# The residual behind w_o turned without its norm, and the norm factor multiplied in later

## The chip, the core and the metric

The kernel runs on one core of a Trainium2 chip. The metric is the device time of one execution in microseconds (us), taken as the median of several executions. All arithmetic is fp32; matrix products are made from split operands, described below.

## What is computed

Two transformer blocks run on 256 tokens of width 2048. The change lies at the end of the second block:

```python
x = x + mixed @ w_o[l]
x = x + peer(rmsnorm(x, norm_ffn_g[l]), peer_wq[l], peer_keys1[l], peer_keys2[l], peer_u[l], peer_v[l])

def rmsnorm(x, g):
    y = x * rsqrt(mean(x * x, axis=-1) + EPS)      # one factor per token
    return y * g                                   # one gain per column

def peer(x, wq, keys1, keys2, u, v):               # per token, 8 heads
    q = x @ wq;  s1 = q[first half] @ keys1;  s2 = q[second half] @ keys2
    # top 16 of s1 and of s2, their 256 sums, top 16 of these: expert numbers and scores
    gate = softmax(top scores)
    act = gelu(x @ u[expert]) * gate
    return act @ v[expert]
```

The kernel does not gather the rows of `u` and `v`. It multiplies all 16,384 experts, as 128 blocks of 128, and puts the gates into a table of tokens and experts that is zero elsewhere. The norm factor of a token (`rstd` below) is one number by which a whole row of x is multiplied, so it can also be multiplied into the scores and into `x @ u` afterwards.

## The kernel before, in words

**Products.** TensorE (PE) multiplies with operands in fp32r, each split in a high and a low part. A stream of 902 units of weights (128x1024) is loaded by the SP queue into four slots. ScalarE (ACT) copies a unit into `w_hi` (`split_hi`, L488), VectorE (DVE) subtracts into `w_lo` (`split_lo`, L497), and PE takes both. Two units are a pair. `ahead` (L507) makes the splits two pairs before PE needs them, and a slot can be split again only when PE has finished the pair that used it. `tokens_out` (L585) makes a 512-column block of a product with tokens on the partitions; `halves_out` (L552) makes a 128-column block with columns on the partitions, first `w_hi` against both activation parts (L561), then `w_lo` against the high part (L568). The stages follow the stream: ..., `heads`, `w_o`, `wqu` (router: per head two pairs of queries and two pairs of expert blocks), `u_decode`, `u_gates`, `u_late`, `v`.

**w_o.** PE makes four column blocks of x (`mix_block`, L2549) in banks 0 to 3. DVE adds each to the residual X (`add_blocks`, L1651), and ACT sums the squares of a block while PE makes the next. In the last block, one token half is finished first, so that its sum, root and reciprocal (`add_last`, `mean_last`, `root_last`, L1931 to L1949) run beside the other half.

**The norm, before.** When w_o has ended, `norm_last` (DVE, L1951) and `norm_second` (ACT, L1113) multiply X by `rstd` into XN, PE turns XN (32 transposes of 128x128, `turn_ffn`, L2588), and ACT and DVE multiply by the gain and split into `act_hi` and `act_lo` (`keep_ffn_hi` L1117, `keep_ffn_lo` L1955). The first query product waits for them tile by tile (`paced` in `halves_out`). The same turning is done earlier in the kernel without the norm, block by block between products, by `turn_block` (L2249), `keep_hi_tiles` (L784) and `keep_lo_tiles` (L1358): the stages w_out and gate use it, and there the norm factor goes into a later step.

**Router.** Per head, ACT copies the queries from their bank and GpSimd (POOL) adds their two halves (`add_copied`, L727, L729); PE multiplies with the keys (`query_scores`, L2615), ACT copies the scores (L1160), and DVE takes the top 16 of each (`top16`, L1983). The two expert blocks of the turn are added on POOL too, and ACT applies Gelu and stores them (`save_early`, L1144).

**u_decode.** 16 expert blocks, numbered 0 to 15 here. Meanwhile DVE turns the picked numbers into expert numbers (L2032 to L2087), with the work of the blocks put between these steps (`more`, L2025): a unit's `split_lo`, and after every second one `add_halves` (L576, L579), which adds the two halves of a block. For a block, ACT waits for this sum, applies Gelu and starts a store (`save_decoded`, L1193), and only then copies the next block's low half (`low_half`, L572) and splits the second unit that DVE wants next. PE starts block n when the sum of block n-2 is made (L2640).

**Scatter.** When the picks are ready, POOL writes the gates of the second 128 tokens into the table in HBM with 128 indirect DMAs (L742). SP waits for all of them before it loads on at the beginning of `u_late` (L642), since it loads the table there.

```python
for n in range(2):                                   # u_decode on ACT, L1182 to L1191
    ahead(split_hi, act, "u_decode", i, 2, n, units=(0,))
    save_decoded(i, n - 1)                           # waits for the sum, Gelu, store
    ...
    low_half(act, GZ[:, n, :], banks[2 + n])
    ahead(split_hi, act, "u_decode", i, 2, n, units=(1,))
```

Of the kernel before, what the change touches and what calls it, by code (L numbers as in the profile page):

```python
# [139 lines left out]
def build(nc, stream, x, p_t, rows, consts, params, rg_w, ukv, keys_t, out):  # L140
    ctx = ExitStack()
    with ctx:
# [108 lines left out]
        RSTD_ROW = at(32512, S)  # L251
        IWORK = at(6200, TT * S).rearrange("p (t n) -> p t n", t=TT)
# [111 lines left out]
        normed_s = sem("normed_s")  # L364
# [169 lines left out]

        def ffn_chunk(k):
            return banks[(4, 5, 6, 7, 2, 3, 1, 4)[k // 2]][:, k % 2 * S:k % 2 * S + S]
# [134 lines left out]
        def _(pool):  # L671
# [58 lines left out]

            with pool.Fori(0, PH) as h:
                for a in range(2):
                    pool.wait_ge(ps_made[a], h + 1)
                    add_copied(PQS[:, a, :], QUERY_HALVES[:, a, :], h * 4 + a)
                for n in range(2):
                    add_copied(Z_HALVES[:, n, 0:S], Z_HALVES[:, n, :], h * 4 + (2 + n))
# [16 lines left out]
        def _(act):  # L753
# [154 lines left out]
            def split_and_square(part, base, i):  # L908

                for k in range(15 if part == "w_o" else 16):  # L910
                    ahead(split_hi, act, part, 0, 8, k)
                    if part == "w_out" and k == 6:

                        act.wait_ge(softplus_ready, 1)
                        act.activation(sp_b, sp_a, ACT.Exp, scale=-1.0).then_inc(softplus_ready, 1)
                    if k >= 4 and k % 4 == 1:
                        if part == "w_out":
                            keep_hi_tiles(1, pa("gate_gain"), gate_in_hi, k // 4 - 1)
                        block_squares(added, base, k // 4 - 1)
# [184 lines left out]
            for t in range(TT):  # L1104
                act.wait_ge(added[1], 8 + t)
                act.activation(XN[:, t, 1536:2048], X[:, t, 1536:2048], ACT.Square,
                               accum_out=ss4[:, 4 * t + 3:4 * t + 4]).then_inc(squares, 1)
                act.wait_ge(mean_ready, 5 + t)
                act.activation(std[:, t:t + 1], ss[:, t:t + 1], ACT.Sqrt).then_inc(std_ready, 1)
                if not t:  # L1110
                    ahead(split_hi, act, "w_o", 0, 8, 15, units=(0,))

            def norm_second(cc):  # L1113
                cols = slice(cc * 512, (cc + 1) * 512)
                act.activation(XN[:, 1, cols], X[:, 1, cols], ACT.Copy, scale=rstd[:, 1:2]).then_inc(normed_s, 1)

            def keep_ffn_hi(chunks):  # L1117
                gain = pa("ffn_gain")
                for k in chunks:
                    act.wait_ge(turned, 3 * KT + k // 2 * 2 + 2)  # L1120
                    act.activation(act_hi[:, k, :], ffn_chunk(k), ACT.Copy, scale=gain[:, k:k + 1])\
                       .then_inc(act_hi_ready, 1)
# [30 lines left out]
            def router_turn(h, first=False):  # L1153
                def keep_query(a):
                    copy_halves(QUERY_HALVES[:, a, :], banks[a], pair_of("wqu", h, 4, a), h * 4 + a, 4)

                def keep_scores(a):
                    act.wait_ge(ps_made[a], h + 2)
                    act.wait_ge(ps_used[a], h + 1)
                    act.activation(PS[:, a, :, :].rearrange("p t n -> p (t n)"), banks[4 + a][:, 0:S],  # L1160
                                   ACT.Copy).then_inc(ps_kept[a], 1)

                ahead(split_hi, act, "wqu", h, 4, 0)
                keep_query(0)
# [3 lines left out]
                keep_query(1)  # L1168
                keep_scores(0)
# [23 lines left out]
            def save_decoded(i, n):  # L1193
                wait_summed(act, block_of("u_decode", i, 2, n))
# [21 lines left out]
            def save_gelu(i, n):  # L1216
                wait_summed(act, block_of("u_gates", i, 2, n))
# [27 lines left out]
            def late_turn(i, first=False):  # L1245
                for n in range(2):
# [9 lines left out]
                    wait_summed(act, block_of("u_late", i, 2, n))  # L1256
# [80 lines left out]
        def _(dve):  # L1337
# [313 lines left out]
            def add_blocks(part, first_banks=(0, 2)):  # L1651

                for b in range(4):
                    n = b % 2
                    for k in range(3):
                        ahead(split_lo, dve, part, 0, 8, 4 * b + k)
                        if part == "w_out" and b and k == 1:
                            keep_lo_tiles(2, pa("gate_gain"), gate_in_hi, gate_in_lo, b - 1)
                        if part == "w_out" and (b, k) == (1, 2):
                            softplus()  # L1660
# [290 lines left out]
            def norm_last(t, cc):  # L1951
                cols = slice(cc * 512, (cc + 1) * 512)
                dve.tensor_scalar(XN[:, t, cols], X[:, t, cols], rstd[:, t:t + 1], None, ALU.mult).then_inc(normed, 1)

            def keep_ffn_lo(chunks):  # L1955
                gain = pa("ffn_gain")
                for k in chunks:
                    dve.wait_ge(act_hi_ready, 4 * KT + k // 2 * 2 + 2)
                    dve.scalar_tensor_tensor(out=act_lo[:, k, :], in0=ffn_chunk(k), scalar=gain[:, k:k + 1],
                                             in1=act_hi[:, k, :].bitcast(F32), op0=ALU.mult, op1=ALU.subtract)\  # L1960
                       .then_inc(act_lo_ready, 1)

# [4 lines left out]
            dve.wait_ge(added[1], 8)  # L1967
            norm_last(0, 0)
            add_last(1)
            for cc in range(1, 4):  # L1970
                norm_last(0, cc)
            mean_last(1)
            root_last(1)
            dve.wait_ge(added[1], 9)
            norm_last(1, 0)
            norm_last(1, 1)
            keep_ffn_lo(range(8))
            ahead(split_lo, dve, "w_o", 0, 8, 15, units=(0,))
            keep_ffn_lo(range(8, 16))
# [132 lines left out]

            def gates_turn(i, last=False):
                for n in range(2):
# [5 lines left out]
                    add_gates(i, n)  # L2120

# [5 lines left out]
            with dve.Fori(GATED, EARLY // 2 - 2 * PH) as i:  # L2127
                for n in range(2):
                    ahead(split_lo, dve, "u_gates", i, 2, n)
                    add_halves(dve, GZ[:, n, :], banks[2 + n], block_of("u_gates", i, 2, n))  # L2130
            for n in range(2):
# [3 lines left out]
            def late_turn(i):  # L2135
                for n in range(2):
                    ahead(split_lo, dve, "u_late", i, 2, n)
                    add_halves(dve, GZ[:, n, :], banks[2 + n], block_of("u_late", i, 2, n))
                    dve.wait_ge(gelu_ready[n], i + (EARLY // 2 + 1) + 1)
# [95 lines left out]
        def _(pe):  # L2235
# [13 lines left out]
            def turn_block(turn, b, taken):  # L2249
                pe.wait_ge(taken[b % 2], b // 2 * 2 + 3)  # L2250
# [313 lines left out]
            mix_block(0, 1)  # L2564
            pe.wait_ge(added[0], 7)
            mix_block(1, 0)
            pe.wait_ge(added[1], 7)
            mix_block(1, 1, range(6))
# [19 lines left out]
            def turn_ffn(t, chunks):  # L2588
                for k in chunks:
                    ins = pe.transpose(ffn_chunk(k)[:, t * P:(t + 1) * P], XN[:, t, k * P:(k + 1) * P], ident)  # L2590
                    if t:
                        ins.then_inc(turned, 1)

            pe.wait_ge(added[0], 9)
            for cc in range(4):
                pe.wait_ge(normed, 4 + cc + 1)
                if cc == 3:
                    pe.wait_ge(added[1], 9)
                turn_ffn(0, range(4 * cc, min(4 * cc + 4, 14)))
            for cc in range(2):  # L2600
                pe.wait_ge(normed, 8 + cc + 1)
                turn_ffn(1, range(4 * cc, 4 * cc + 4))
            pe.wait_ge(normed_s, 1)
            turn_ffn(1, range(8, 12))
            pe.wait_ge(normed_s, 2)
            turn_ffn(1, range(12, 14))
            pe.wait_ge(act_lo_ready, 4 * KT + 2)
            turn_ffn(0, range(14, 16))
            turn_ffn(1, range(14, 16))

            def queries_out(h, a, paced=False):
                pe.wait_ge(copied, h * 4 + (a + 1))
                halves_out(pe, pair_of("wqu", h, 4, a), odd_of("wqu", a), banks[a], paced=4 * KT if paced else None)
# [12 lines left out]
            queries_out(0, 0, paced=True)  # L2626
            queries_out(0, 1)
            pe.wait_ge(table_ready, 32)
# [215 lines left out]
```

## Time and profile before

| | us |
|---|---|
| three runs of the kernel | 2696.3, 2696.33, 2696.57 (median 2696.33) |
| the profiled execution | 2696.89 |
| its span, first to last instruction | 2695.2 |
| PE busy in the span | 2669.4 (99%) |
| DVE busy | 1835.3 (68%) |
| ACT busy | 1369.4 (51%) |
| POOL busy | 371.4 (14%) |

The times below are in us from the start of the span of the profiled execution. A line of the timeline gives a start, a length, the engine, the line of the kernel, what is written from what, how many instructions are merged, and in brackets how long the engine stood idle before and who ended that. Lengths of PE overlap, since matmuls are pipelined; what a matmul costs is read from one start to the next. The span is 1.7 below the execution's own time.

### The profile page before, as it was taken

The numbers are of one execution on the slowest core, as the hardware profiler recorded it, in microseconds if no ns is written. First come the engines' busy times: TensorE is split into PE (matmuls) and PEld (weight loads), VectorE is DVE, ScalarE is ACT, GpSimd is POOL, SyncE is SP. The second block draws the span as 40 slices with busy tenths as digits, with TensorE's granted clock in tenths as the row PEclk, the third lists the DMA queues.
The fourth block names the chain that finished last, engine by engine and source line by source line (L and its number), as shares of the span: only waits on it lengthen the run. The fifth ranks groups of instructions, "written<-read, shape, count | busy, mean of one in ns | idle before, by whom it ended". The sixth has DMA issues, their size and how long they took to land.

```text
span 2695.2 us, 47112 instructions
## 1 busy us (share of the span) xinstructions
PE 2669.4 (99%) x14299; PEld 2298.4 (85%) x14299; DVE 1835.3 (68%) x2985; ACT 1369.4 (51%) x2066; POOL 371.4 (14%) x296
## 2 busy tenths in 40 slices
PE   8999999999999999999999999999999999999998
PEld 6888888898888998888888888888888888888887
DVE  6666665668987677489996777775565555555555
ACT  6454445555665444455455555554444444444444
POOL 0010000001011211011105555551000000000000
PEclk9999999999999999999999999999999999999999
DMA  7566555564554554655567777777976666666564
GB/s 257 189 216 213 181 199 177 177 219 159 172 176 156 167 168 157 195 201 186 195 201 212 202 202 203 201 204 218 305 240 217 217 217 219 212 220 216 200 241 156
DMA packets 204475, 543.26 MB, mean 202 GB/s; under 512 B 37504, under 2 KB 82816, under 8 KB 203392
## 3 DMA queue, kind: packets, MB, share of 16 engines
q1 hardware_dynamic: 148112, 486.74, 54.9%
q10 hardware_dynamic: 35568, 47.33, 5.0%
q0 software_dynamic: 20736, 8.46, 2.7%
q8 instruction: 30, 0.49, 0.1%
q14 instruction: 29, 0.24, 0.0%
HBM read 515.12 MB, written 27.33 MB: 201 GB/s over the span
## 4 chain that ended last, share of the span: by engine, by line
PE 94%; DVE 3%; ACT 1%; issue 1%; DMA 0%; SPq 0%; DVEq 0%; POOL 0%; ACTq 0%; POOLq 0%
PE bank L561 32%; PE bank L568 16%; PE bank L2693 8%; PE bank L2694 8%; PE bank L2695 8%; PE bank L601 4%; PE bank L603 4%; PE bank L602 4%; PE bank L2488 1%; DVE w_lo L504 1%; PE bank L527 1%; PE bank L528 1%; PE bank L529 1%; PE bank L2658 1%; PE bank L2465 0%
## 5 line engine op out<-in xcount | busy, mean ns | idle before, releaser
L504 DVE TENSOR_TENSOR w_lo<-raw,w_hi 128x1024 fp32r<-128x1024 f32 x902 | 1097.9, 1226 | 725.9 <-ACT w_hi L495 719.4
L495 ACT ACTIVATE w_hi<-raw 128x1024 fp32r<-128x1024 f32 x902 | 950.8, 1059 | 946.5 <-PE bank L568 363.1
L561 PE MATMUL bank<-act,w_hi 128*128 128x512 f32 x3840 | 975.2, 396 | 2.6 <-DVE cst L579 1.0
L561 PEld LDWEIGHTS bank<-act,w_hi 128*128 128x128 f32 x3840 | 692.0, 189 | 133.8 <-issue 6.4
L568 PEld LDWEIGHTS bank<-act,w_lo 128*128 128x128 f32 x3840 | 519.7, 190 | 33.1
L568 PE MATMUL bank<-act,w_lo 128*128 128x256 f32 x3840 | 535.6, 282 | 0.0
L2693 PE MATMUL bank<-w_hi,expert_act 128*128 128x512 f32 x1008 | 392.3, 389 | 0.1
L2694 PE MATMUL bank<-w_lo,expert_act 128*128 128x512 f32 x1008 | 392.2, 389 | 0.0
L2695 PE MATMUL bank<-w_hi,expert_act 128*128 128x512 f32 x1008 | 392.1, 389 | 0.0
L742 POOL DMA_INDIRECT g_kept<-slot_t x128 | 239.7, 1872 | 253.8 <-issue 170.4
L2693 PEld LDWEIGHTS bank<-w_hi,expert_act 128*128 128x128 f32 x1008 | 189.3, 188 | 39.6 <-DVE cst L579 0.5
L2695 PEld LDWEIGHTS bank<-w_hi,expert_act 128*128 128x128 f32 x1008 | 189.3, 188 | 39.3
L2694 PEld LDWEIGHTS bank<-w_lo,expert_act 128*128 128x128 f32 x1008 | 189.3, 188 | 39.1
L601 PE MATMUL bank<-w_hi,act 128*128 128x512 f32 x320 | 125.8, 393 | 2.0 <-DVE act L1401 1.1
L603 PE MATMUL bank<-w_hi,act 128*128 128x512 f32 x320 | 124.7, 390 | 0.0
L602 PE MATMUL bank<-w_lo,act 128*128 128x512 f32 x320 | 124.6, 389 | 0.0
L748 POOL TENSOR_TENSOR big<-big 128x1024 f32<-128x1024 f32 x2 | 5.8, 2878 | 839.4 <-DVE big L2196 839.4
L601 PEld LDWEIGHTS bank<-w_hi,act 128*128 128x128 f32 x320 | 60.1, 188 | 16.2 <-DVE w_lo L504 1.3
L603 PEld LDWEIGHTS bank<-w_hi,act 128*128 128x128 f32 x320 | 60.1, 188 | 12.6
L602 PEld LDWEIGHTS bank<-w_lo,act 128*128 128x128 f32 x320 | 60.1, 188 | 12.1
L729 POOL TENSOR_TENSOR big<-big 128x256 f32<-128x256 f32 x32 | 33.1, 1034 | 248.3 <-ACT big L1138 248.3
L2107 DVE SCALAR_TENSOR_TENSOR weighted<-cst,slot_t 128x256 fp32r<-128x256 f32 x128 | 61.3, 479 | 0.0
(344 smaller groups left out, 2498.4 us busy)
## 6 DMA issues: line engine op xcount, KB each, us to landing
raw<-in_stream SPq DMA_DIRECT2D x902, 512.0 KB
z_kept<-cst ACTq DMA_DIRECT2D x112, 128.0 KB, 2.4
cst<-z_kept ACTq DMA_DIRECT2D x112, 128.0 KB, 3.9
g_kept<-zeros POOLq DMA_DIRECT2D x16, 512.0 KB
big<-in_ukv ACTq DMA_DIRECT2D x16, 512.0 KB, 4.6
big<-g_kept SPq DMA_DIRECT2D x16, 512.0 KB, 5.6
big<-in_rows ACTq DMA_DIRECT2D x3, 1024.0 KB, 5.8
big<-in_x SPq DMA_DIRECT2D x2, 1024.0 KB, 10.2
```

Source lines behind the costliest of these rows:

```text
L495: act.activation(w_hi[:, s, :], raw[:, s, :], ACT.Copy).then_inc(hi_ready, 1)
L504: dve.tensor_tensor(w_lo[:, s, :], raw[:, s, :], w_hi[:, s, :].bitcast(F32), ALU.subtract).then_inc(lo_ready, 1)
L561: pe.matmul(bank[:, :], w_hi[:, s, kk * P:(kk + 1) * P], act2[:, k, :, :].rearrange("p a n -> p (a n)"), start=(k == 0), stop=False)
L568: mm = pe.matmul(bank[:, 0:S], w_lo[:, s, kk * P:(kk + 1) * P], act_hi[:, k, :], start=False, stop=(k == KT - 1))
L601: pe.matmul(outs[t], a_hi, hi, start=(k == 0), stop=False)
L602: pe.matmul(outs[t], a_hi, lo, start=False, stop=False)
L603: mm = pe.matmul(outs[t], a_lo, hi, start=False, stop=(k == KT - 1))
L742: pool.indirect_dma_start(g_kept, bass.IndirectOffsetOnAxis(ap=SLOT_INDEX[:, i:i + 1], axis=0), SLOT_GATE[:, i:i + 1], None, compute_op=AL ...
L2107: dve.scalar_tensor_tensor(out=weighted[:, tile, :, :], in0=iota.unsqueeze(1).broadcast_to([P, 2, P]), scalar=first_index[:, bass.ds(tok, 1)],
L2693: pe.matmul(o, a_hi, hi, start=first, stop=False, skip_group_check=True)
L2694: pe.matmul(o, a_hi, lo, start=False, stop=False, skip_group_check=True)
L2695: mm = pe.matmul(o, a_lo, hi, start=False, stop=False, skip_group_check=True)
```

## The change

- `norm_last`, `norm_second`, `turn_ffn`, `keep_ffn_hi` and `keep_ffn_lo` go. X itself is turned by `turn_block`: blocks 0, 1 and 2 in the middle of w_o's next block, block 3 between the two units of the first query pair (`first_queries`). ACT and DVE keep its tiles with `keep_hi_tiles` and `keep_lo_tiles`, blocks 0 to 2 during w_o, block 3 behind it. On ACT and DVE the first unit of the pair after the first query pair is now split before block 3's tiles.
- DVE makes two diagonals of `rstd`; PE multiplies them with ones, which gives a row of `rstd` on every partition (two matmuls between the second query pair and the first scores), and ACT keeps it as `FFN_ROW`.
- Scores are multiplied by `rstd` while ACT copies them, in two instructions per copy instead of one.
- Expert blocks are multiplied by `FFN_ROW` (128x256) before Gelu: on POOL in the router and in `u_decode`, on DVE in `u_gates` and `u_late`. ACT waits for the multiplied block. POOL's loop over `u_decode` stands ahead of the scatter.

```diff
+            def early_block(n, block):
+                z = Z_HALVES[:, n, 0:S]
+                pool.wait_ge(copied, block + 5)
+                step(pool.tensor_tensor(z, z, Z_HALVES[:, n, S:2 * S], ALU.add))
+                pool.wait_ge(row_kept, 2)
+                step.wait()
+                pool.tensor_tensor(z, z, FFN_ROW, ALU.mult).then_inc(pool_summed, 1)
...
+            with pool.Fori(0, PH) as i:
                 for n in range(2):
-                    add_copied(Z_HALVES[:, n, 0:S], Z_HALVES[:, n, :], h * 4 + (2 + n))
+                    wait_summed(pool, block_of("u_decode", i, 2, n))
+                    pool.tensor_tensor(GZ[:, n, :], GZ[:, n, :], FFN_ROW, ALU.mult).then_inc(z_scaled, 1)
             pool.wait_ge(picks_ready, 5)
...
-            act.wait_ge(rstd_ready, 7)
-            norm_second(2)
-            keep_ffn_hi(range(4))
-            norm_second(3)
-            keep_ffn_hi(range(4, 8))
+            ahead(split_hi, act, "w_o", 0, 8, 15, units=(0,))
+            keep_hi_tiles(3, pa("ffn_gain"), act_hi, 3)
             ahead(split_hi, act, "w_o", 0, 8, 15, units=(1,))
-            keep_ffn_hi(range(8, 16))
...
-                    act.activation(PS[:, a, :, :].rearrange("p t n -> p (t n)"), banks[4 + a][:, 0:S],
-                                   ACT.Copy).then_inc(ps_kept[a], 1)
+                    for t in range(TT):
+                        kept = act.activation(PS[:, a, t, :], banks[4 + a][:, t * P:(t + 1) * P], ACT.Copy,
+                                              scale=rstd[:, t:t + 1])
+                    kept.then_inc(ps_kept[a], 1)
...
             def save_decoded(i, n):
-                wait_summed(act, block_of("u_decode", i, 2, n))
+                act.wait_ge(z_scaled, i * 2 + (n + 1))
...
             ahead(split_lo, dve, "w_o", 0, 8, 15, units=(0,))
-            keep_ffn_lo(range(8, 16))
+            keep_lo_tiles(4, pa("ffn_gain"), act_hi, act_lo, 3)
+            step(dve.memset(ONES, 1.0))
+            for t in range(TT):
+                step(dve.tensor_scalar(RSTD_DIAG[:, t, :], ident, rstd[:, t:t + 1], None, ALU.mult))
+            step.wait()
+            dve.sem_inc(rstd_ready, 1)
             ahead(split_lo, dve, "w_o", 0, 8, 15, units=(1,))
...
+            def scale_rows(n, block):
+                wait_summed(dve, block)
+                dve.tensor_tensor(GZ[:, n, :], GZ[:, n, :], FFN_ROW, ALU.mult).then_inc(z_scaled, 1)
...
-            mix_block(0, 1)
+            mix_block(0, 1, range(4))
+            turn_block(2, 0, added, 4)
+            mix_block(0, 1, range(4, 8))
...
+            def first_queries():
+                pe.wait_ge(copied, 1)
+                pe.wait_ge(added[1], 8)
+                pe.wait_ge(act_lo_ready, 4 * KT + 12)
+                halves_out(pe, pair_of("wqu", 0, 4, 0), odd_of("wqu", 0), banks[0], units=(0,))
+                turn_block(2, 3, added, 4)
+                halves_out(pe, pair_of("wqu", 0, 4, 0), odd_of("wqu", 0), banks[0], units=(1,), paced=4 * KT)
...
+            pe.wait_ge(rstd_ready, 8)
+            for t in range(TT):
+                ins = pe.matmul(banks[6][:, t * P:(t + 1) * P], ONES, RSTD_DIAG[:, t, :], start=True, stop=True)
+            ins.then_inc(row_made, 1)
```

## Rows read from the trace of the kernel before

**Rows 1.** Stretches: length, then busy time of PE, PEld, DVE, ACT, POOL (instructions), clock, DMA.

```profile
1152.30:1166.20 13.90, 11.28 (x65) 8.38 (x65) 12.15 (x29) 10.49 (x24) 0.00 (x0) 1.00 0.45 164
1166.20:1346.60 180.40, 180.40 (x1058) 159.46 (x1057) 160.10 (x445) 91.55 (x124) 32.33 (x31) 1.00 0.59 196
1346.60:1438.75 92.15, 91.06 (x518) 79.34 (x516) 79.77 (x105) 55.20 (x77) 12.91 (x8) 1.00 0.68 205
1438.75:1625.00 186.25, 186.25 (x1088) 164.57 (x1087) 138.22 (x257) 99.32 (x160) 102.11 (x56) 1.00 0.74 203
1900.50:1990.50 90.00, 90.00 (x520) 79.28 (x519) 56.90 (x81) 45.49 (x66) 0.00 (x0) 1.00 0.90 289
```

**Rows 2.** Timeline of PE from w_o's last product to the second query pair.

```profile
1151.92 0.39 PE L2582 MATMUL bank<-w_hi,mix_lo 128*128 128x512 f32 x1
...
1158.86 2.28 PE L561 MATMUL bank<-act,w_hi 128*128 128x512 f32 x8
...
1166.20 2.00 PE L561 MATMUL bank<-act,w_hi 128*128 128x512 f32 x8
```

**Rows 3.** Timeline of PE in w_out: a block of eight transposes between products.

```profile
400.90 0.40 PE L603 MATMUL bank<-w_hi,act 128*128 128x512 f32 x1
401.14 1.04 PE L2256 MATMUL bank<-cst,big 128*128 128x128 f32 x8
401.93 0.47 PE L601 MATMUL bank<-w_hi,act 128*128 128x512 f32 x1
```

**Rows 4.** Timeline of ACT and DVE behind w_o: the last root, and four tiles on each.

```profile
1154.54 0.20 ACT L1109 ACTIVATE stat<-stat 128x1 f32<-128x1 f32 x1 [0.72 <-DVE stat L1943]
1155.99 1.57 ACT L1121 ACTIVATE act<-bank,par 128x256 fp32r<-128x256 f32 x4 [0.30 <-PE bank L2590]
1156.87 1.66 DVE L1959 SCALAR_TENSOR_TENSOR act<-bank,par,act 128x256 fp32r<-128x256 f32 x4 [1.01 <-ACT act L1121]
```

**Rows 5.** Timeline of PE: the first scores and the product behind them.

```profile
1171.79 0.61 PE L2620 MATMUL bank<-big 128*128 128x128 f32 x4
1172.15 2.09 PE L561 MATMUL bank<-act,w_hi 128*128 128x512 f32 x8
```

**Rows 6.** Waits of DVE in the router, 1166 to 1346: total, times, longest.

```profile
DVE w_lo L504 <- ACT w_hi L495: 13.3, 24, 1.6
```

**Rows 7.** Timeline of DVE and PE in u_decode.

```profile
1357.70 0.42 DVE L579 TENSOR_TENSOR cst<-cst,bank 128x256 f32<-128x256 f32 x1
1361.89 2.28 DVE L2053 TENSOR_TENSOR big<-big,cst 128x2048 f32<-128x2048 f32 x1
1409.83 0.41 DVE L579 TENSOR_TENSOR cst<-cst,bank 128x256 f32<-128x256 f32 x1
1410.38 2.10 PE L561 MATMUL bank<-act,w_hi 128*128 128x512 f32 x8 [0.15 <-DVE cst L579]
```

**Rows 8.** Timeline of ACT in u_decode: Gelu of a block, then the next split.

```profile
1380.03 0.42 ACT L1195 ACTIVATE cst<-cst 128x256 f32<-128x256 f32 x1 [0.85 <-DVE cst L579]
...
1381.41 1.06 ACT L495 ACTIVATE w_hi<-raw 128x1024 fp32r<-128x1024 f32 x1
```

**Rows 9.** Timeline of POOL and DVE where both are busy, in the rnn stage.

```profile
621.83 2.39 POOL L701 TENSOR_TENSOR ckvt_lo<-big,ckvt_hi 128x1024 fp32r<-128x1024 f32 x1 [320.72 <-DVE big L1772]
622.25 3.05 DVE L504 TENSOR_TENSOR w_lo<-raw,w_hi 128x1024 fp32r<-128x1024 f32 x1
...
624.18 1.62 POOL L706 TENSOR_TENSOR big<-big 128x256 f32<-128x256 f32 x1
```

**Rows 10.** Lines L719 and L742 on POOL and L504 on DVE: length min/median/max in ns, first and last start.

```profile
L719 POOL TENSOR_TENSOR big<-big x32: 734/738/742, 818.5 to 1068.2; 128x256 f32<-128x256 f32 x32
L504 DVE TENSOR_TENSOR w_lo<-raw,w_hi x902: 1203/1225/3053, 5.9 to 2678.0; 128x1024 fp32r<-128x1024 f32 x181
L742 POOL DMA_INDIRECT g_kept<-slot_t x128: 1552/1576/2657, 1416.6 to 1841.3; - x128
```

**Rows 11.** Timeline of SP: the first load behind its wait for the scatter.

```profile
1878.76 0.34 SPq L619 DMA_DIRECT2D raw<-in_stream  x1
```

More of the change, by code:

```diff
@@ L729, in add_copied @@
                 pool.tensor_tensor(dest, halves[:, 0:S], halves[:, S:2 * S], ALU.add).then_inc(pool_summed, 1)
-            with pool.Fori(0, PH) as h:
-                for a in range(2):
-                    pool.wait_ge(ps_made[a], h + 1)
-                    add_copied(PQS[:, a, :], QUERY_HALVES[:, a, :], h * 4 + a)
+            def early_block(n, block):
[5 more added lines that the diff above has]
+                pool.tensor_tensor(z, z, FFN_ROW, ALU.mult).then_inc(pool_summed, 1)
+            with pool.Fori(0, PH) as h:
+                with step.turns(h, 2, PH):
+                    for a in range(2):
+                        pool.wait_ge(ps_made[a], h + 1)
+                        add_copied(PQS[:, a, :], QUERY_HALVES[:, a, :], h * 4 + a)
+                    for n in range(2):
+                        early_block(n, h * 4 + (2 + n))
+            with pool.Fori(0, PH) as i:
                 for n in range(2):
-                    add_copied(Z_HALVES[:, n, 0:S], Z_HALVES[:, n, :], h * 4 + (2 + n))
+                    wait_summed(pool, block_of("u_decode", i, 2, n))
+                    pool.tensor_tensor(GZ[:, n, :], GZ[:, n, :], FFN_ROW, ALU.mult).then_inc(z_scaled, 1)
             pool.wait_ge(picks_ready, 5)
@@ L1168, in router_turn @@
                 keep_query(1)
+                if first:
+                    act.wait_ge(row_made, 2)
+                    act.activation(FFN_ROW, banks[6][:, 0:S], ACT.Copy).then_inc(row_kept, 1)
+                    act.wait_ge(rstd_ready, 7)
                 keep_scores(0)
@@ L1658, in add_blocks @@
                             keep_lo_tiles(2, pa("gate_gain"), gate_in_hi, gate_in_lo, b - 1)
+                        if part == "w_o" and b and k == 1:
+                            keep_lo_tiles(4, pa("ffn_gain"), act_hi, act_lo, b - 1)
                         if part == "w_out" and (b, k) == (1, 2):
@@ L1949, in root_last @@
                 dve.wait_ge(rstd_ready, 6 + t)
[L1951 to L1961, printed above, removed]
             dve.wait_ge(added[0], 9)
@@ L2120, in gates_turn @@
                     add_gates(i, n)
+                    scale_rows(n, block_of("u_gates", i, 2, n))
             dve.wait_ge(scattered, 16 * ZERO_DMAS)
@@ L2130, in _ @@
                     add_halves(dve, GZ[:, n, :], banks[2 + n], block_of("u_gates", i, 2, n))
+                    scale_rows(n, block_of("u_gates", i, 2, n))
             for n in range(2):
@@ L2138, in late_turn @@
                     add_halves(dve, GZ[:, n, :], banks[2 + n], block_of("u_late", i, 2, n))
+                    scale_rows(n, block_of("u_late", i, 2, n))
                     dve.wait_ge(gelu_ready[n], i + (EARLY // 2 + 1) + 1)
@@ L2563, in _ @@
             pe.wait_ge(added[1], 5)
-            mix_block(0, 1)
+            mix_block(0, 1, range(4))
+            turn_block(2, 0, added, 4)
+            mix_block(0, 1, range(4, 8))
             pe.wait_ge(added[0], 7)
-            mix_block(1, 0)
+            mix_block(1, 0, range(4))
+            turn_block(2, 1, added, 4)
+            mix_block(1, 0, range(4, 8))
             pe.wait_ge(added[1], 7)
-            mix_block(1, 1, range(6))
+            mix_block(1, 1, range(4))
+            turn_block(2, 2, added, 4)
+            mix_block(1, 1, range(4, 6))
             pair = pair_of("w_o", 0, 8, 15)
@@ L2586, in _, with queries_out @@
                     mm.then_inc(bank_done, 1)
[L2588 to L2611, printed above, removed]
-                pe.wait_ge(copied, h * 4 + (a + 1))
-                halves_out(pe, pair_of("wqu", h, 4, a), odd_of("wqu", a), banks[a], paced=4 * KT if paced else None)
+            def queries_out(h, a):
+                pe.wait_ge(copied, h * 4 + (a + 1))
+                halves_out(pe, pair_of("wqu", h, 4, a), odd_of("wqu", a), banks[a])
+            def first_queries():
[5 more added lines that the diff above has]
+                halves_out(pe, pair_of("wqu", 0, 4, 0), odd_of("wqu", 0), banks[0], units=(1,), paced=4 * KT)
             def query_scores(h):
```

36 lines of the change are left out of this document (9 added, 27 removed).

## The prediction, made before the changed kernel was run

> **What bounds the kernel now.** The page comes first: PE is busy in nearly the whole span, so a change is worth what it takes from, or adds to, PE's path. The table of stretches says where that isn't so. PE has no idle time in the router, in u_gates and in u_late; between w_o and the router it is idle for 2.6 of 13.9 us, and in u_decode for 1.1 of 92.15 us [rows 1]. The change touches exactly these two places: it shortens the first and puts a step into the second. The timeline of the first shows w_o's last product at 1151.92 and the second query pair at 1166.20 [rows 2]. The timeline of the second shows DVE without a pause, and a PE that waits 0.15 us for a block's sum by DVE [rows 7]: there DVE sets the pace, not PE.
>
> Terms are differences within the profiled execution (2696.89 us, 0.56 above the median of the runs); I add them to the median, 2696.33. A measurement of this kernel can tell some 0.2%, 5.4 us, from no change.
>
> **1. What goes behind w_o.** Products start 0.24 apart [rows 3], so w_o leaves PE at 1152.16; up to 1166.20 are 14.04 us. The first query pair in it needs what the second takes, 1166.20 to 1171.79, 5.59 us [rows 2, 5]. Saved: 8.45 us, the 32 transposes, the waits for the norm and the paced tiles together.
>
> **2. What comes in its place.** A block of eight transposes between products costs 0.79 from its start to the next product's, which is 0.07 longer than usual [rows 3]: 0.86. Three blocks in w_o: 2.6. They wait for nothing: a block of X is summed half a w_o block earlier, and w_out does the same now. ACT's and DVE's twelve tiles there take 0.39 and 0.42 each [rows 4], beside PE. The fourth block costs 0.86 and holds up the second half of the query pair: root at 1154.54, then ACT's split of 1.06 [rows 4, 8], which now stands before the tiles, then DVE's of 1.23 [rows 10], then four tiles of 0.42. That puts the last tile at 1158.3 (DVE's norm steps ahead of the root are gone) to 1158.7, and the pair's end some 1.3 later (its last product and its low half, an estimate), at 1159.6 to 1160.0, against 1152.16 + 5.59 + 0.86 = 1158.6 without a wait. I take 1.1, bounds 0 (the engines get there first) and 2.5 (both chains one after the other). The two matmuls for the row of factors cost what two such matmuls of the scores do, 0.36 plus 0.09 of the next product [rows 5]: 0.45. Sum: 8.45 - 2.6 - 0.86 - 1.1 - 0.45 = **3.4 saved**, between 2.0 and 4.5.
>
> **3. Edits costed at nothing.** Scores in two ACT instructions, and the router's second POOL step per block: ACT is busy for half of the router, and DVE still waits 13.3 us for ACT's splits there [rows 1, 6], 1.7 per head; POOL's step may take some 1 us of that from DVE. Were that cover gone, it would be up to 8 us. DVE's 0.42 per block in u_gates and u_late: DVE is busy for 138.2 of 186.25 and 56.9 of 90 us [rows 1], and what waits for the scaled block, Gelu, is wanted only a pair later. SP's queue is not moved.
>
> **4. What the change adds in u_decode.** ACT's Gelu now waits for DVE's sum and then POOL's multiplication. The shape on POOL takes 0.74 [rows 10]. This is short, but it does not run beside DVE. In the rnn stage POOL subtracts for 2.39 us; DVE's split, begun meanwhile, takes 3.05 instead of 1.23, and POOL's next step, behind that split, takes 1.62 [rows 9, 10] for a shape that elsewhere takes 0.74. Each waits until the other has finished, and the one that waits goes first. The Trainium skill says the same on its page "SBUF — State Buffer", section "Who interferes with whom": a VectorE instruction with two SBUF inputs and a GpSimd instruction that reads SBUF exclude each other, and the second to issue is blocked until the first has finished. By that rule each multiplication costs DVE most of its own length, and the sum is the one below; without it, it is the first rival's. The 3.05 and the 1.62 agree with it.
>
> DVE's work here is such instructions, one behind another: splits, the comparison of 2.28 (L2053), products. From the sum of block 0 to that of block 9, 1357.70 to 1409.83, it does not rest [rows 7]. After each of the nine sums before the last, POOL stands behind DVE's next instruction, then holds the one after it. I take 0.6 for each (0.74 less the overlap that instructions have): 5.4. After block 0, DVE's split waits for ACT's, which waits for Gelu: 0.2 more than the hold; and after the four L2053 POOL starts 2.2 late, Gelu with it, and ACT's split is done 2.44 after Gelu's start [rows 8], just when DVE wants it: 0.4 in all. DVE's chain comes **6.0** later to block 9's sum, and PE, which waits for that sum today [rows 7], too. From block 10 on the picks are nearly done and DVE has pauses again. Bounds: 0.8 (no collision, only the step's length, once) and 7.5 (nine full 0.74 and more of ACT's lateness).
>
> **Sum:** 6.0 - 3.4 = +2.6. Forecast **2698.9 us**; by the bounds of both terms, 2696.3 to 2701.8. This is no change that can be measured, made of two that could nearly be.
>
> **Rivals.** *No collision.* POOL's reads don't hold DVE's products (only splits are seen to be held [rows 9]), or DVE's chain has more air than it seems. Then u_decode costs 0.8 to 1.5 and the time is 2693.8 (2692 to 2695.5). For it: sums of blocks on POOL in the router leave no mark on PE. Against: rows 9.
>
> *DVE keeps the port: slower.* If POOL gets in only when DVE stops, then after L2053 nothing but two-input instructions follows until DVE waits for the split that hangs on POOL. Place: blocks 1, 3, 5, 7. Price: 0.74 + 2.44 of rest each, 12.7, and some 3.3 for the others: 16 in place of 6, so 2709. It decides if POOL is passed over once per block. Against: in rows 9 the engine that waited was served first, though there it was DVE.
>
> *The scatter comes too late: slower.* POOL's loop over u_decode now stands before it. It began at 1416.6; it can begin when block 15 is multiplied, some 4 us behind the end of u_decode at 1438.75 [rows 1], so 26 later. It ended its last start at 1841.3 [rows 10], some 5 us before it had landed (estimate); with 26 more, 1872. SP's load behind the wait goes out at 1878.76 [rows 11]: 6 us of room, and about 6 more until PE misses the unit. It decides if the scatter's 425 us become 3% longer; at 5%, 9 us: 2708.
>
> *The fourth block costs as much as the norm did.* Then the first term is 0 to 1 and the time 2702.
>
> **How the numbers follow.** Forecast 0.50, no collision 0.26, DVE keeps the port 0.11, late scatter 0.04, fourth block 0.04, 0.05 for a gain I don't see. The range of 2692 to 2703 leaves out the third, the fourth and the last, 0.20; the forecast's own is 2696.3 to 2701.8. Faster than 2690.9 needs more than the whole bound of the first term: 0.06. Slower than 2701.7: the three slow rivals and the edge of the forecast, 0.20. Within: 0.74.
>
> **What would show it.** Right: the second query pair begins some 7.8 us behind the start of w_o's last product (0.24 + 5.59 + 0.86 + 1.1), where it was 14.3; w_o is 2.6 longer; in u_decode DVE instructions with two SBUF inputs are 0.6 longer behind each sum, POOL's multiplication takes 0.7 to 3 us, and block 0 to block 9 takes 58 us instead of 52.1; PE waits for L579 more than now. Wrong: L2053, L2062 and L504 keep their lengths in u_decode (no collision); DVE idle for 3 us before L504 at every second block (port kept); SP waiting for the scatter near 1879; or PE idle behind w_o for more than 2.5 us.

## The result, and the profile of the changed kernel

The changed kernel takes 2700.15 us (median of 19 runs, the shortest 2699.07), the one before 2696.42: a ratio of 1.0019, 95% interval 1.0013 to 1.0025. This is 3.7 us, where 2.6 were forecast, and less than the 5.4 us by which "no change" was bounded. It is the case that the prediction called likeliest: a gain behind w_o and a larger loss in u_decode. The profiled execution took 2699.15 us (span 2697.5). Four of the 19 runs, called long below, took 2706.22 to 2711.17 us, and one of the kernel before 4458.5, so medians are compared.

First the table of stretches, cut at the same places of the work as [rows 1] (behind w_o up to the second query pair, router, u_decode, u_gates; columns as there):

```profile
1153.85:1161.36 7.51, 7.19 (x41) 5.69 (x40) 5.08 (x13) 5.34 (x10) 0.00 (x0) 1.00 0.39 156
1161.36:1342.25 180.89, 180.89 (x1062) 159.94 (x1061) 160.89 (x446) 95.76 (x141) 43.97 (x46) 1.00 0.60 202
1342.25:1440.64 98.39, 92.05 (x518) 79.50 (x517) 86.11 (x105) 54.98 (x77) 22.91 (x17) 1.00 0.58 191
1440.64:1627.26 186.62, 186.35 (x1088) 164.56 (x1087) 148.68 (x288) 99.35 (x160) 102.66 (x56) 1.00 0.74 203
```

Behind w_o 7.51 us stand where 13.90 stood, and PE is idle for 0.32 of them, not for 2.6. u_decode takes 98.39 instead of 92.15, and PE, which was idle for 1.1 us of it, now is for 6.3.

The timeline of PE behind w_o, which answers to [rows 2] and [rows 5]:

```profile
1153.62 0.39 PE L2583 MATMUL bank<-w_hi,mix_lo 128*128 128x512 f32 x1
1153.85 1.98 PE L559 MATMUL bank<-act,w_hi 128*128 128x512 f32 x8
...
1156.62 1.04 PE L2251 MATMUL bank<-cst,big 128*128 128x128 f32 x8
1157.41 1.17 PE L559 MATMUL bank<-act,w_hi 128*128 128x512 f32 x4
1158.89 1.68 PE L559 MATMUL bank<-act,w_hi 128*128 128x512 f32 x4 [0.32 <-DVE act L1365]
...
1161.36 2.00 PE L559 MATMUL bank<-act,w_hi 128*128 128x512 f32 x8
...
1166.95 0.61 PE L2616 MATMUL bank<-big 128*128 128x128 f32 x4
1167.40 0.61 PE L2606 MATMUL bank<-big 128*128 128x128 f32 x4
```

The last product of w_o begins at 1153.62, the second query pair at 1161.36: 7.74 us, where the prediction said 7.8 and the kernel before took 14.3. The fourth block's transposes stand at 1156.62 and the one wait for its tiles at 1158.89. The two matmuls for the row of factors take 0.45, from 1166.95 to the first scores.

Then u_decode. DVE's timeline, from the sum of block 0 to that of block 9 (L577 is the sum, L505 the split, L2041 and L2050 the comparison and the products), which answers to [rows 7]; POOL's own; and the split and the products of the kernel before:

```profile
1353.31 0.41 DVE L577 TENSOR_TENSOR cst<-cst,bank 128x256 f32<-128x256 f32 x1
...
1371.77 2.28 DVE L2041 TENSOR_TENSOR big<-big,cst 128x2048 f32<-128x2048 f32 x1
1373.97 1.76 DVE L505 TENSOR_TENSOR w_lo<-raw,w_hi 128x1024 fp32r<-128x1024 f32 x1
1375.65 1.28 DVE L2050 TENSOR_TENSOR big<-big 128x512 f32<-128x512 f32 x2
1377.18 1.22 DVE L505 TENSOR_TENSOR w_lo<-raw,w_hi 128x1024 fp32r<-128x1024 f32 x1 [0.25 <-ACT w_hi L496]
1378.32 0.41 DVE L577 TENSOR_TENSOR cst<-cst,bank 128x256 f32<-128x256 f32 x1
1378.65 1.83 DVE L2050 TENSOR_TENSOR big<-big 128x512 f32<-128x512 f32 x2
...
1411.72 0.41 DVE L577 TENSOR_TENSOR cst<-cst,bank 128x256 f32<-128x256 f32 x1
```

```profile
1371.93 2.72 POOL L747 TENSOR_TENSOR cst<-cst,par 128x256 f32<-128x256 f32 x1 [5.43 <-DVE cst L577]
1378.81 1.12 POOL L747 TENSOR_TENSOR cst<-cst,par 128x256 f32<-128x256 f32 x1 [4.17 <-DVE cst L577]
```

```profile
1376.10 1.22 DVE L504 TENSOR_TENSOR w_lo<-raw,w_hi 128x1024 fp32r<-128x1024 f32 x1
...
1379.91 1.29 DVE L2062 TENSOR_TENSOR big<-big 128x512 f32<-128x512 f32 x2
```

Block 0 to block 9 takes 58.41 us; it was 52.13. Read the first two fences together. POOL is released by the sum and issues at 1371.93, 0.16 behind the start of L2041; it ends only at 1374.65, for it stands still until L2041 is done. Now the split of 1373.97 stands still for POOL: 1.76 in place of 1.22. In the next block POOL meets a product, whose pair takes 1.83 in place of 1.28. Each of the first nine multiplications holds DVE for some 0.55 us; this is called a hold below. Five times DVE also waits for ACT's split, as at 1377.18, because Gelu came late: 0.22, 0.27, 0.25, 0.25 and 0.24. The Gelu ahead of that split was released by POOL:

```profile
1374.68 0.42 ACT L1196 ACTIVATE cst<-cst 128x256 f32<-128x256 f32 x1 [4.75 <-POOL cst L747]
```

The waits of 1340 to 1460 (total, times, longest) say the same from the other side; behind them, PE's in the same stretch of the kernel before:

```profile
ACT cst L1196 <- POOL cst L747: 30.1, 14, 4.8
...
PE bank L559 <- DVE cst L577: 6.2, 8, 1.0
```

```profile
PE bank L561 <- DVE cst L579: 1.0, 4, 0.4
```

Last, the scatter on POOL, its first and its last start, and SP's first load behind the wait for it, which answer to [rows 10] and [rows 11]; and the one wait of ACT for that load:

```profile
1444.79 1.80 POOL L753 DMA_INDIRECT g_kept<-slot_t  x1 [0.22 <-issue]
...
1882.66 2.50 POOL L753 DMA_INDIRECT g_kept<-slot_t  x1 [0.30 <-issue]
```

```profile
1886.74 0.81 SPq L617 DMA_DIRECT2D raw<-in_stream  x2
```

```profile
ACT w_hi L496 <- DMA raw<-in_stream: 1.9, 1, 1.9
```

The scatter starts 28.2 us later and its last DMA 41.4 later, for it also takes 437.9 us from first to last start where it took 424.7. SP's load was due at 1881.0 (1878.76, and 2.26 for the later place of the whole kernel) and goes out at 1886.74. ACT waits 1.9 us for what it brings; PE has no wait there yet.

### The profile page after: what moved, and what is told of

Its sections match the earlier page's. It is cut to its first block, busy times and chain, and to the rows that moved or that the text cites. A ratio compares the mean times of both kernels' runs of the same rounds, so it can differ in the third digit from the quotient of the medians.

```text
span 2697.5 us, 47398 instructions
## 1 busy us (share of the span) xinstructions
PE 2669.1 (99%) x14303; PEld 2299.3 (85%) x14303; DVE 1874.8 (70%) x3078; ACT 1372.0 (51%) x2081; POOL 407.3 (15%) x328
## 4 chain that ended last, share of the span: by engine, by line
PE 83%; issue 12%; POOL 2%; DVE 1%; ACT 1%; DMA 0%; POOLq 0%; SPq 0%; DVEq 0%; ACTq 0%
PE bank L559 26%; PE bank L566 14%; PE bank L2683 8%; PE bank L2685 8%; PE bank L2684 8%; PE bank L599 4%; PE bank L601 3%; PE bank L600 3%; PE bank L2483 1%; PE bank L528 1%; PE bank L529 1%; PE bank L530 1%; POOL big L727 1%; POOL big L732 1%; PE bank L2648 1%
## 5 line engine op out<-in xcount | busy, mean ns | idle before, releaser
L505 DVE TENSOR_TENSOR w_lo<-raw,w_hi 128x1024 fp32r<-128x1024 f32 x902 | 1100.4, 1230 | 687.7 <-ACT w_hi L496 670.8
L2143 DVE TENSOR_TENSOR expert_act<-big,expert_act 128x256 fp32r<-128x256 f32 x128 | 53.6, 420 | 0.8 <-ACT expert_act L1263 0.8
```

The costliest lines, as they stand in the source:

```text
L505: dve.tensor_tensor(w_lo[:, s, :], raw[:, s, :], w_hi[:, s, :].bitcast(F32), ALU.subtract).then_inc(lo_ready, 1)
```

## Experiments

All are run beside the kernel before on the same chip; its median was 2696.4 to 2696.7 each time. The diffs show the lines that matter; `...` stands for lines left out, among them the counts of semaphores that follow from the edit. In experiments 1 to 4 and 7 the norm factor of u_decode's blocks is left out.

**1. Without the multiplication in u_decode.** POOL's loop is taken out, Gelu waits for the sum.

```diff
-    with pool.Fori(0, PH) as i:
-        for n in range(2):
-            wait_summed(pool, block_of("u_decode", i, 2, n))
-            pool.tensor_tensor(GZ[:, n, :], GZ[:, n, :], FFN_ROW, ALU.mult).then_inc(z_scaled, 1)
...
 def save_decoded(i, n):
-    act.wait_ge(z_scaled, i * 2 + (n + 1))
+    wait_summed(act, block_of("u_decode", i, 2, n))
...
```

> The changed kernel without the multiplication of u_decode's sixteen blocks by the row of factors; ACT's Gelu waits for DVE's sum again and POOL's scatter starts as soon as the picks are ready. It leaves out the norm factor of these blocks. My theory, that the part behind w_o gives 3.4 us and everything that is lost is lost in u_decode: block 0's sum to block 9's takes 52.1 us again instead of 58.4, the scatter starts some 4 us earlier than in the kernel before, and the time is 2693.0 (2692.0 to 2694.2), with no run some us above the others. Rival, that the late start is an accident of the profiled run and the part behind w_o gives nothing: 2696. Rival, that u_gates' and u_late's multiplications on DVE cost as well: 2694.5 or more.

Measured: 2693.16 us, ratio 0.9989 (0.9980 to 0.9998); block 0 to block 9 in 51.88 us. So the part behind w_o gives 3.3 us net in time (by the interval, 0.5 to 5.4), and the changed kernel loses through u_decode's multiplication. DVE's multiplications in u_gates and u_late show no cost.

**2. The same with the late scatter.** One wait more on POOL, for the sum of u_decode's last block.

> As the kernel without the multiplication in u_decode, but POOL waits for the sum of u_decode's last block before it scatters, as the changed kernel makes it. Norm factor of u_decode's blocks left out. If the late scatter is what made 4 of 19 runs of the changed kernel 6 to 11 us longer, then most runs stay within 1 us of the kernel without the multiplication (2693) and about one in five is 5 to 11 us above that; the scatter ends about 28 to 41 us later than with the early start. If those long runs have another cause (the multiplication itself, the first stages), no run here is more than 3 us above the median.

Measured: 2693.09 us, ratio 0.9987 (0.9978 to 0.9996), 11 runs from 2691.98 to 2693.87. The scatter began at 1437.85, 25 us later than in experiment 1, but its last start was at 1854.28, only 23 later, and SP's load was not held. No run is long, where the expectation had about one in five: by its own words this speaks for another cause of the long runs, though 11 runs are few.

**3. POOL beside DVE, nobody waiting.** On experiment 1, POOL multiplies the row of factors by itself into an unused tile after each of the first ten sums.

```diff
+    for k in range(10):
+        wait_summed(pool, block_of("u_decode", 0, 2, k))
+        pool.wait_ge(z_scaled, k)
+        pool.tensor_tensor(GB[:, k % 2, :], FFN_ROW, FFN_ROW, ALU.mult).then_inc(z_scaled, 1)
...
```

> As the kernel without the multiplication, but POOL multiplies two unrelated inputs of 128x256 into an unused tile after each of u_decode's first ten sums; nobody waits for it there. Norm factor of u_decode's blocks left out. My theory, that POOL and DVE hold each other: each of DVE's splits or products behind a sum is 0.55 longer, block 0's sum to block 9's takes 52.1 + 9 x 0.55 = 57.0 us, and the time is 2693.0 + 4.9 = 2697.9 (2696.5 to 2698.5). Rival, that what costs in u_decode is the longer chain from sum to Gelu and not the port: 52.1 to 52.7 us, DVE's instructions keep their lengths, 2693.0 to 2693.6.

Measured: 2697.33 us, ratio 1.0004 (0.9995 to 1.0013); block 0 to block 9 in 55.60. DVE's timeline and POOL's:

```profile
1371.51 2.28 DVE L2041 TENSOR_TENSOR big<-big,cst 128x2048 f32<-128x2048 f32 x1
1373.71 1.63 DVE L505 TENSOR_TENSOR w_lo<-raw,w_hi 128x1024 fp32r<-128x1024 f32 x1
1375.27 1.28 DVE L2050 TENSOR_TENSOR big<-big 128x512 f32<-128x512 f32 x2
...
1377.94 1.70 DVE L2050 TENSOR_TENSOR big<-big 128x512 f32<-128x512 f32 x2
```

```profile
1371.67 2.60 POOL L747 TENSOR_TENSOR cst<-par 128x256 f32<-128x256 f32 x1 [5.42 <-DVE cst L577]
1378.09 0.99 POOL L747 TENSOR_TENSOR cst<-par 128x256 f32<-128x256 f32 x1 [3.83 <-DVE cst L577]
```

The same two instructions are held, by 0.42 (1.63 and 1.70), with no wait for ACT anywhere between them: nine times 0.42 are 3.8 us, and the stretch grew by 3.7. My 4.9 was worked out with the 0.55 of the changed kernel. The rival, that only the longer chain costs, is out. That the hold is 0.42 and not 0.55 goes with POOL's own instruction, which takes 0.61 alone, not 0.74, when both inputs are the same tile. Nearly all that is left of the changed kernel's 6.28 is 9 x 0.13, or 1.2, and the 1.23 of waits for ACT.

**4. The same with one input.** As experiment 3, with a multiplication by a constant. This changes POOL's operation as well (TENSOR_SCALAR).

```diff
-        pool.tensor_tensor(GB[:, k % 2, :], FFN_ROW, FFN_ROW, ALU.mult).then_inc(z_scaled, 1)
+        pool.tensor_scalar(GB[:, k % 2, :], FFN_ROW, 2.0, None, ALU.mult).then_inc(z_scaled, 1)
```

> As the kernel with POOL's unrelated multiplication of two inputs, but POOL multiplies one input of 128x256 by a constant. Norm factor of u_decode's blocks left out. With two inputs DVE's next instruction was 0.42 longer, POOL's own 0.61 less some 0.19. If any read of SBUF by POOL holds DVE's two-input instructions: a hold of POOL's length less 0.19, block 0's sum to block 9's 51.9 + 9 times that, 2693.2 + the same less 0.7. If only POOL's two-input instructions hold: 51.9 us, DVE's lengths unchanged, 2693.2.

Measured: 2694.94 us, ratio 0.9994 (0.9985 to 1.0003); 53.71 us. Neither: DVE is held, but by 0.20 only, although POOL's instruction is the longest of the three (0.85 alone, and 1.23 behind a product). This run does not tell apart whether the number of inputs or the operation makes the hold short. The lines:

```profile
1373.63 1.42 DVE L505 TENSOR_TENSOR w_lo<-raw,w_hi 128x1024 fp32r<-128x1024 f32 x1
...
1377.64 1.48 DVE L2050 TENSOR_TENSOR big<-big 128x512 f32<-128x512 f32 x2
```

```profile
1377.80 1.23 POOL L747 TENSOR_SCALAR cst<-par 128x256 f32<-128x256 f32 x1 [3.38 <-DVE cst L577]
...
1408.82 0.85 POOL L747 TENSOR_SCALAR cst<-par 128x256 f32<-128x256 f32 x1 [4.97 <-DVE cst L577]
```

**5. The multiplication on DVE**, right behind each sum; the scatter starts early again. POOL's loop is taken out.

```diff
...
                     add_halves(dve, GZ[:, pair % 2, :], banks[2 + pair % 2], block_of("u_decode", 0, 2, pair))
+                    scale_rows(pair % 2, block_of("u_decode", 0, 2, pair))
...
```

> The changed kernel with u_decode's multiplication on DVE, right behind each sum, instead of on POOL; the scatter starts as soon as the picks are ready. My theory: DVE's chain gets 0.33 to 0.42 us for each of nine blocks and no holds; ACT's Gelu comes 0.4 later instead of 0.7 to 2.7, so little of the 0.25 waits stays: block 0's sum to block 9's takes 55.1 to 56.2 us instead of 58.4, the time is 2696.0 to 2697.3, and no run lies 5 us or more above the median if the late scatter made those. Rival, that the cost is the step itself wherever it runs: 58 us and 2699 to 2700.

Measured: 2698.44 us, ratio 1.0008 (0.9999 to 1.0017), 1.1 us above my range; block 0 to block 9 in 56.03, inside it, at its upper end. Each step costs 0.46, not 0.33, because DVE must see its own sum finished:

```profile
1377.50 0.42 DVE L577 TENSOR_TENSOR cst<-cst,bank 128x256 f32<-128x256 f32 x1
1377.95 0.42 DVE L2005 TENSOR_TENSOR cst<-cst,par 128x256 f32<-128x256 f32 x1
1378.30 1.29 DVE L2051 TENSOR_TENSOR big<-big 128x512 f32<-128x512 f32 x2
```

From sum to multiplication are 0.45, where a following instruction that waits for nothing comes 0.33 later. Of the rest that the forecast lacked, 0.4 is a wait of PE for a tile of DVE's (`weighted`) at the start of u_gates, which experiment 1 does not have, and 0.4 lies outside the span: the execution is 2.1 longer than its span here, and 1.7 there. No run is long (2697.49 to 2699.82).

**6. The changed kernel again, and with the early scatter alone.** In the second, POOL multiplies blocks 0 to 9, DVE 10 to 15.

> The changed kernel once more, unchanged, beside the variants: 2699.5 to 2700.5 most of the time. If the long runs (4 of 19, 6 to 11 us above the others) belong to this kernel, one to four of these runs are some 5 to 11 us longer again; if they belonged to the hour in which they were taken, none is.

> The changed kernel with POOL multiplying u_decode's blocks 0 to 9 only and DVE blocks 10 to 15, so that the scatter starts as soon as the picks are ready, some 25 us earlier than in the changed kernel. The holds stay: block 0's sum to block 9's takes 58.3 us, the time is 2699.3 (2698.6 to 2700.3). If it is the late scatter, together with POOL's multiplications, that makes some runs of the changed kernel 6 to 11 us longer, no run here is; if the multiplications alone do it, some are.

Measured: 2700.42 (ratio 1.0018, 1.0009 to 1.0027) and 2700.04 (1.0012, 1.0003 to 1.0022). The holds are worth the same with either scatter: PE waits 6.6 and 6.5 us for the sums. Of the first kernel's 11 runs two were long again (2707.1 and 2707.9), so 6 of 30 in all; of the second's none (at most 2702.05). An early start is not an early end, though: in the second's profiled run the scatter began at 1420.07 and took 457.6 us to its last start at 1877.64, which is 0.8 behind that of the first's (1876.81). SP waits 2.2 and 2.1 us for it there, and PE waits in neither for what that load brings.

**7. The scatter later still**, on experiment 1: POOL waits for the eighth block of u_gates.

> As the kernel without the multiplication in u_decode, but POOL begins its scatter only behind the eighth block of u_gates, some 45 us later than in the kernel with the late scatter (1437.9 there). Norm factor of u_decode's blocks left out. The scatter took 413 to 460 us in the runs so far, so it ends at 1896 to 1943. If a scatter that ends too late holds up SP's load and so PE, as the rival said, SP's load waits for it, PE is idle in u_late for the first time, and the time is 2693.1 plus what the end lies behind some 1890: 2700 to 2745, with a spread of many us between runs. If the load has more room than that, or the scatter gets faster by itself: 2693.

Measured: 2731.39 us, four runs from 2720.44 to 2748.56. PE and SP in u_late, then the stretches around it (PE, PEld, DVE, ACT, POOL, clock, DMA):

```profile
1884.69 1.11 PE L566 MATMUL bank<-act,w_lo 128*128 128x256 f32 x8
1940.13 3.54 PE L559 MATMUL bank<-act,w_hi 128*128 128x512 f32 x8 [54.33 <-ACT cst L1216]
```

```profile
1935.26 0.82 SPq L617 DMA_DIRECT2D raw<-in_stream  x2
```

```profile
1850.00:1900.00 50.00, 35.80 (x206) 31.35 (x204) 19.24 (x24) 15.72 (x24) 28.61 (x16) 0.89 0.48 110
1900.00:1950.00 50.00, 9.87 (x48) 8.48 (x49) 5.79 (x7) 5.39 (x8) 20.31 (x13) 0.57 0.40 98
1950.00:2000.00 50.00, 50.00 (x288) 43.96 (x288) 33.81 (x50) 25.14 (x36) 0.00 (x0) 1.00 0.96 308
```

PE stops at 1885.80 and runs again 4.87 us after SP's load goes out. By this delay it would not have stopped had the load gone out by 1880.9 (an estimate). The changed kernel stands some 6 us later (spans 2697.5 and 2691.5 of experiment 1), so there the limit is near 1887, again an estimate; its load went out at 1886.74. PE comes back slowly, too: the first eight products take 3.54 us, the next eight of the same kind 2.00 as before. The granted clock is 0.57 from 1900 to 1950, in which PE was idle for 40 us, so mostly the lower of its two levels (1.2 and 2.4 GHz); from 1950, with PE busy, it is 1.00.

**8. The picks' decoding spread over more blocks**, with the multiplication on DVE: five half units of u_decode for each of the four rounds instead of four. The first kernel puts the fifth between the products:

```diff
...
-                        if h % 2:
+                        if h - half * heads in (0, 1, 3):
                             more()
...
```

> As the kernel with u_decode's multiplication on DVE, and the decoding of the picks spread over five half units of u_decode for each of its four rounds instead of four, so that it ends some two blocks later. DVE then has 14.5 us of work for 2.5 blocks, which take PE 14.0, where it had 12.9 for two, which take 11.2. My theory, that only DVE's pace in the first nine blocks costs anything: PE's waits for the sums fall from 4.2 us to under 1.5, the time is 2694.3 (2693.3 to 2695.8), under both kernels. Rival, that the multiplication costs as a step, not by DVE's pace: 2697.5 to 2698.5 as without the spreading.

The second, the even one, puts it behind the reduction instead:

```diff
                     step(dve.tensor_reduce(PICK[:, a, half * heads:(half + 1) * heads, :, :]
...
-                    more()
+                    more(2)
...
```

> As the kernel with DVE's multiplication and the decoding spread over five half units, but with the additional half unit behind each reduction (L2055's line), so that two long steps no longer stand in one block. Most DVE work between two sums is then 6.6 us where it was 7.5, against 5.6 of PE. Theory of DVE's pace: PE's waits for the sums fall from 2.6 us to 1.0 to 1.6, the time is 2694.4 (2693.4 to 2695.4). Rival: the order inside a round makes no difference, 2695.4.

Measured: 2695.36 (ratio 0.9998, 0.9989 to 1.0007, one run of 2705.34) and 2693.96 (0.9992, 0.9983 to 1.0001). Both lie in their ranges. PE's waits for the sums fall from 4.2 us to 2.6, less than I said, since a reduction and a comparison met in one block (sums at 1369.22 and 1376.67, 7.45 apart), and in the even one to

```profile
PE bank L559 <- DVE cst L577: 1.1, 3, 0.6
```

The even one beats the changed kernel by 6 us, and all its 11 runs lie under the median of the kernel before (at most 2696.07); its interval still reaches 1.0001.

**9. Two controls.** The even one with each multiplication behind the next split, and the kernel before with the spreading of experiment 8's first kernel alone.

```diff
...
                 ahead(split_lo, dve, "u_decode", 0, 2, pair, units=(u,))
+                if not u and pair:
+                    scale_rows((pair - 1) % 2, block_of("u_decode", 0, 2, pair - 1))
...
```

> As the evenly spread kernel, but each block's multiplication on DVE stands behind the next half unit's split, so that DVE need not wait until its own sum has left the engine (0.12 us of each 0.46). Theory: 16 x 0.12 us less of DVE, PE's waits 0.3 to 1.0 us, 2694.0 (2693.1 to 2695.0). Rival, that Gelu, now 1.2 us later, comes too late for ACT's next split, as it did behind POOL: waits of 0.25 of DVE for ACT appear again and the time is that of the evenly spread kernel or more.

> The kernel before with nothing but the decoding of the picks spread over five half units, to tell apart what the spreading gives by itself. PE's idle time in u_decode was 1.1 us, which is all there is to win: 2695.4 (2694.8 to 2696.4). If it gives more than that, the gain of the spread kernels is not that of the part behind w_o.

Measured: 2711.89 (1.0061, 1.0048 to 1.0074), and 2696.56 (1.0007, 0.9997 to 1.0016). The first is the rival's, and much dearer than I thought (waits of 1350 to 1440):

```profile
ACT cst L1192 <- DVE cst L2005: 34.1, 12, 4.5
...
PE bank L559 <- DVE cst L577: 12.3, 9, 2.3
```

ACT does its next split behind Gelu. Gelu waits for the multiplication, the multiplication stands behind DVE's split, and that waits for ACT's split before it: a ring, in which block 0 to block 15 takes 101.8 us where the even one takes 83.7. The second gives nothing that can be measured and lies 0.2 above my range; PE still waits 1.4 us for the sums, 1.0 before. The even spreading was not run by itself, but it has only the 1.1 us of PE's idle time in u_decode to win, and the even kernel gains 2.5 with the multiplication in it: the part behind w_o must be in that gain.

## Why the prediction was right, and where it was off

**Behind w_o.** By the trace, the three blocks in w_o cost 2.7 (w_o's last product 1.70 later, though this execution was 0.98 ahead when w_o began, with the heads' last pair at 1059.62, at 1060.60 before; forecast 2.6). The fourth block's stall is 1.06: from 1153.85, with 5.59 and 0.86 the second pair would begin at 1160.30, and it begins at 1161.36 (forecast 1.1). The row's matmuls cost 0.45, as said. First product behind the first scores: 1167.76, and 1172.15 before [rows 5], 4.39 earlier, 0.98 of that from the start: 3.41 saved, forecast 3.4. Experiment 1 gives 3.3 in time. The rival of the dear fourth block is out.

**u_decode.** 6.28 for a forecast of 6.0. The holds were 9 x 0.55 = 4.95, forecast 5.4; the waits for ACT 1.23, forecast 0.6: the one after block 0 was 0.22 for 0.2, the four after the comparisons 1.01 for 0.4. The two errors nearly cancel, which is luck. The order was as argued: the engine that waits goes first, so POOL is never passed over for two instructions, and *DVE keeps the port* is out; the holds put *no collision* out. By the rule of the Trainium skill, page "SBUF — State Buffer", section "Who interferes with whom", a POOL instruction that reads SBUF and a DVE instruction with two SBUF inputs exclude each other: the traces agree on the exclusion. But the hold is shorter than the length that the profile gives POOL's instruction (0.55 of 0.74; 0.20 of 0.85 with one input), and there the measurement decides.

**Costed at nothing.** The router takes 180.89 us (180.40 before, 0.45 of it the row's matmuls), and DVE waits 13.1 us for ACT there, 13.3 before. What I missed is small: at the start of u_gates PE waits 0.27 for a tile of DVE's (`weighted`), whose first step takes 0.66 beside POOL's last multiplication and 0.27 the next time; experiment 1 has no such wait. There the changed kernel falls another 0.37 behind. By parts: -3.41 + 6.28 + 0.37 = 3.2 us; the medians say 3.7, and the 0.5 between them was not traced. The prediction called the change too small to measure; with 19 runs of each kernel the interval leaves out 1. Its lower bound does not follow from its terms: 0.8 lost and 4.5 saved give 2692.6, not 2696.3; the range of 2692 to 2703 has room for that.

**The late scatter**, given 0.04. Its place and its price were right; the size of one term was not. I let the scatter start 26 us later and keep its length; it starts 28 later, and the length is not a constant: over the profiled runs it took 410 to 458 us from first to last start. In the profiled run it was 3.1% longer, and the rival was to decide from 3%. So the profiled run sits on the edge, and 6 of 30 runs of this kernel are 6 to 11 us longer, as the rival had it. Whether the scatter made those six is open. For it: experiment 7 shows that a scatter that ends late enough stops PE, and experiment 6 had no such run in 11 with the early start. Against it: experiment 2 had none in 11 with the late one, and both kernels of experiments 8 and 9 with the first spreading, whose scatter begins some 10 us late, had one (2705.34 in 11 and 2711.53 in 12). No long run was caught in a trace.

## What to carry to other kernels

A multiplication on POOL is not free beside a DVE that never rests: price it as a hold on the instruction of DVE's that it meets (here 0.2 to 0.55 us, and none on a reduction), and count what it makes late behind itself. If such a step must go where DVE sets the pace, first spread DVE's other work. A job moved behind a loop on its queue has a deadline elsewhere: compute the room from the job's longest run, not from the one in the profile.

## What I had not expected of the hardware

POOL's length does not give the hold: 0.55 us with two tiles as inputs (0.74 alone), 0.42 with the same tile twice (0.61 alone), but 0.20 with one input and a constant (0.85 alone). The first two are 0.19 below the length; the third is the longest instruction and the shortest hold, with another operation as well as one input less. Nor is it a matter of DVE's two inputs alone. In DVE's timeline of the changed kernel L2029, which has one input, takes 0.84 while POOL multiplies, and its twin L2028 0.29 (both took 0.29 in the kernel before); but the reduction of L2060 and POOL's multiplication behind block 9 overlap, neither is longer, and only the split behind them is:

```profile
1353.64 0.29 DVE L2028 TENSOR_SCALAR big<-big 128x256 uint32<-128x256 uint32 x1
1353.85 0.84 DVE L2029 TENSOR_SCALAR big<-big 128x256 uint32<-128x256 uint32 x1
...
1412.05 0.41 DVE L2060 TENSOR_REDUCE stat<-big 128x16 f32<-128x256 f32 x1
1412.38 1.65 DVE L505 TENSOR_TENSOR w_lo<-raw,w_hi 128x1024 fp32r<-128x1024 f32 x1
```

```profile
1353.81 0.73 POOL L747 TENSOR_TENSOR cst<-cst,par 128x256 f32<-128x256 f32 x1 [7.06 <-DVE cst L577]
...
1412.21 0.74 POOL L747 TENSOR_TENSOR cst<-cst,par 128x256 f32<-128x256 f32 x1 [5.42 <-DVE cst L577]
```

And a job of DMAs issued by POOL, the same 128 in every kernel, took between 410 and 458 us from first to last start over the 14 profiled runs, with nothing in the profile that tells in advance which.
